# Two transformer blocks on one Trainium2 core: the four feed-forwards issue their TensorE products in four other forms

## The reference

```
x = layer_norm(a * x + 0.5 * swiglu_ffn(x, ffn_w_in[i, 0], ffn_w_out[i, 0]), ...)
x = layer_norm(a * x + mixer(x), ...)
x = layer_norm(a * x + memory_cross_attention(x, mem, ...), ...)
x = layer_norm(a * x + 0.5 * swiglu_ffn(x, ffn_w_in[i, 1], ffn_w_out[i, 1]), ...)

def swiglu_ffn(x, w_in, w_out):
    h = x @ w_in                  # 1024 -> 2 * 2816
    g, u = jnp.split(h, 2, axis=-1)
    return (jax.nn.silu(g) * u) @ w_out   # 2816 -> 1024
```

## Time and profile before

| | |
|---|---|
| runs shown | 3226.77, 3240.44 and 3244.69 us; median 3240.44 us |
| profiled execution | span 3246.9 us, 58680 instructions (the page states no other time of it; first to last instruction) |
| PE busy | 3078.8 us, 95% of the span, 24248 instructions |
| PEld busy | 2819.9 us, 87%, 24248 instructions |
| POOL, DVE, ACT busy | 1351.4 us (42%), 1128.6 us (35%), 1121.9 us (35%) |
| TensorE clock granted, mean | 0.974 of full |

### The profile page before, as it was taken

The page is one execution under the profiler, slowest core; times in us unless marked ns, Lnnn a source line. Parts: engine busy times, 40 slices in busy tenths (PEclk is TensorE's granted clock), DMA queues, the critical chain, the costliest instruction groups (busy, mean ns, idle before and its releaser), DMA issues.

```text
span 3246.9 us, 58680 instructions
## 1 busy us (share of the span) xinstructions
PE 3078.8 (95%) x24248; PEld 2819.9 (87%) x24248; DVE 1128.6 (35%) x1881; ACT 1121.9 (35%) x1894; POOL 1351.4 (42%) x648
## 2 busy tenths in 40 slices
PE   7998998999899999989889999999999999899998
PEld 7986588987488999979479789999999988789997
DVE  1525742534843211152760541102211054541103
ACT  4333733233733222232733332222322244332222
POOL 5434045433134444344036254444554445254443
PEclk9998999999999999999989999999999999999999
DMA  5211023212012232222013122232222332122231
GB/s 191 72 66 52 1 68 115 72 46 73 13 52 93 90 103 97 91 77 92 14 52 121 62 78 90 90 104 84 84 95 99 100 113 86 46 84 91 99 102 58
DMA packets 72059, 261.19 MB, mean 80 GB/s; under 512 B 8016, under 2 KB 8656, under 8 KB 70896
## 3 DMA queue, kind: packets, MB, share of 16 engines
q1 hardware_dynamic: 69728, 249.77, 23.0%
q10 hardware_dynamic: 2192, 9.44, 0.8%
HBM read 257.09 MB, written 2.10 MB: 80 GB/s over the span
## 4 chain that ended last, share of the span: by engine, by line
PE 86%; DVE 8%; ACT 2%; issue 2%; POOL 1%; DMA 0%; ACTq 0%; DVEq 0%; POOLq 0%
PE bank L524 25%; PE bank L506 16%; PE bank L510 16%; PE bank L508 16%; PE bank L664 1%; PE bank L837 1%; PE bank L869 1%; PE bank L853 1%; PE bank L1078 1%; DVE small L2187 1%; PE bank L1069 1%; PE bank L715 1%; POOL wl L392 1%; DVE tb L1819 1%; PE bank L907 1%
## 5 line engine op out<-in xcount | busy, mean ns | idle before, releaser
L392 POOL TENSOR_TENSOR wl<-raw,wh 128x1024 fp32r<-128x1024 f32 x464 | 1151.9, 2497 | 1794.0 <-ACT wh L1182 1793.8
L1182 ACT CAST wh<-raw 128x1024 fp32r<-128x1024 f32 x464 | 472.9, 1049 | 1035.1 <-PE bank L510 804.2
L506 PE MATMUL bank<-xh,wh 128*128 128x256 f32 x3168 | 641.6, 284 | 0.0
L508 PE MATMUL bank<-xl,wh 128*128 128x256 f32 x3168 | 625.2, 279 | 0.0
L510 PE MATMUL bank<-xh,wl 128*128 128x256 f32 x3168 | 624.9, 279 | 0.0
L506 PEld LDWEIGHTS bank<-xh,wh 128*128 128x128 f32 x3168 | 485.1, 190 | 19.7 <-issue 18.3
L508 PEld LDWEIGHTS bank<-xl,wh 128*128 128x128 f32 x3168 | 483.3, 189 | 0.0
L510 PEld LDWEIGHTS bank<-xh,wl 128*128 128x128 f32 x3168 | 483.3, 189 | 0.0
L524 PE MATMUL bank<-xh,wh 128*128 128x256 f32 x1952 | 394.9, 285 | 53.6 <-ACT xh L1244 37.6
L524 PE MATMUL bank<-xh,wl 128*128 128x256 f32 x1952 | 392.4, 283 | 0.0
L524 PEld LDWEIGHTS bank<-xh,wh 128*128 128x128 f32 x1952 | 305.6, 194 | 64.8 <-issue 64.1
(11 more groups left out here) (338 smaller groups left out, 3797.5 us busy)
## 6 DMA issues: line engine op xcount, KB each, us to landing
raw<-in_slabs SPq DMA_DIRECT2D x464, 512.0 KB, 3.3
h<-in_x_t SPq DMA_DIRECT2D x8, 256.0 KB, 5.5
w1v<-in_w ACTq DMA_DIRECT2D x2, 1024.0 KB, 5.0
side<-in_pp_w ACTq DMA_DIRECT2D x2, 1024.0 KB, 5.2
out<-h SPq DMA_DIRECT2D x8, 256.0 KB, 2.0
side<-in_w SPq DMA_DIRECT2D x1, 1024.0 KB, 12.6
vt<-in_p_t ACTq DMA_DIRECT2D x2, 512.0 KB, 6.5
side<-in_w ACTq DMA_DIRECT2D x1, 1024.0 KB, 7.2
```

Of the source, the lines that this page charges most:

```text
L392: nc.gpsimd.tensor_tensor(wl[:, n % RING, :], raw[:, n % RING, :], wh[:, n % RING, :], A.subtract).then_inc(w_low, 1)
L506: nc.tensor.matmul(dst[:, c], high_l, high_r[:, c], start=first and n == 0, stop=False)
L508: nc.tensor.matmul(dst[:, c], high_l, low_r[:, c], start=False, stop=False)
L1182: nc.scalar.copy(wh[:, slot, :], raw[:, slot, :]).then_inc(w_high, 1)
```

## The change

`columns_of` gives the cuts of a 512-column bank under four names: halves (256 + 256, as before), whole (512), wide_first (280 + 232) and wider_first (320 + 192). `passes`, `part`, `pair` and `products` take a form. The four feed-forwards get:

| feed-forward | ffn_in | ffn_out |
|---|---|---|
| (0, 0) | the first product of each `passes` pair cut 280 + 232, the rest in halves | whole |
| (0, 1) | whole | halves |
| (1, 0) | the first product of each `passes` pair cut 320 + 192, the rest in halves | `by_half`: all three products of one half, then of the other |
| (1, 1) | halves, and ahead of every pair a constant bf16 product of 128 columns into bank 7, which nothing reads | halves |

`first_form` reaches only the `passes` pair of a trip and there only the first product of chunk 0 into the first bank, so it touches 11 products of a stage. All other stages keep their halves.

```
--- before.py
+++ after.py
@@ -497,12 +497,27 @@
 
         @blk.tensor
         def _(pe):
-            def passes(dst, high_l, low_l, high_r, low_r, first, last):
-
-                w = dst.shape[1]
-                cut = w // 2 if w == T else w
-                parts = [slice(a, a + cut) for a in range(0, w, cut)]
+            def columns_of(w, form):
+
+                if w != T:
+                    return [slice(0, w)]
+                at = {"halves": (0, 256, T), "whole": (0, T), "wide_first": (0, 280, T), "wider_first": (0, 320, T)}[form]
+                return [slice(a, b) for a, b in zip(at, at[1:])]
+
+            def by_half(dst, high_l, low_l, high_r, low_r, first, last):
+
+                parts = columns_of(dst.shape[1], "halves")
                 for n, c in enumerate(parts):
+                    nc.tensor.matmul(dst[:, c], high_l, high_r[:, c], start=first and n == 0, stop=False)
+                    nc.tensor.matmul(dst[:, c], high_l, low_r[:, c], start=False, stop=False)
+                    out = nc.tensor.matmul(dst[:, c], low_l, high_r[:, c], start=False,
+                                           stop=last and n == len(parts) - 1)
+                return out
+
+            def passes(dst, high_l, low_l, high_r, low_r, first, last, form="halves", first_form=None):
+
+                parts = columns_of(dst.shape[1], form)
+                for n, c in enumerate(columns_of(dst.shape[1], first_form or form)):
                     nc.tensor.matmul(dst[:, c], high_l, high_r[:, c], start=first and n == 0, stop=False)
                 for c in parts:
                     nc.tensor.matmul(dst[:, c], high_l, low_r[:, c], start=False, stop=False)
@@ -514,18 +529,16 @@
             def tile_of(n, j):
                 return wh[:, n % RING, j * P:(j + 1) * P], wl[:, n % RING, j * P:(j + 1) * P]
 
-            def part(dst, terms, first, last):
-
-                w = dst.shape[1]
-                cut = w // 2 if w == T else w
-                cols = [slice(a, a + cut) for a in range(0, w, cut)]
+            def part(dst, terms, first, last, form="halves"):
+
+                cols = columns_of(dst.shape[1], form)
                 for i, (fixed, moving) in enumerate(terms):
                     for n, c in enumerate(cols):
                         out = nc.tensor.matmul(dst[:, c], fixed, moving[:, c], start=first and i + n == 0,
                                                stop=last and i == len(terms) - 1 and n == len(cols) - 1)
                 return out
 
-            def pair(slab, kind, act_h, act_l, w, high_in=None, low_in=None):
+            def pair(slab, kind, act_h, act_l, w, high_in=None, low_in=None, form="halves", first_form=None):
 
                 banks = [bank[2 * kind + o][:, 0:w] for o in range(2)]
                 for k in range(KC if low_in is None else KC + 1):
@@ -534,21 +547,23 @@
                             high_in(k)
                         for o in range(2):
                             a, b = tile_of(slab + o, k)
-                            last = passes(banks[o], a, b, act_h[:, k, :], act_l[:, k, :], k == 0, k == KC - 1)
+                            last = passes(banks[o], a, b, act_h[:, k, :], act_l[:, k, :], k == 0, k == KC - 1, form,
+                                          first_form if k + o == 0 else None)
                         continue
                     if k < KC:
                         high_in(k)
                         for o in range(2):
                             a, b = tile_of(slab + o, k)
-                            part(banks[o], ((a, act_h[:, k, :]), (b, act_h[:, k, :])), k == 0, False)
+                            part(banks[o], ((a, act_h[:, k, :]), (b, act_h[:, k, :])), k == 0, False, form)
                     if k:
                         low_in(k - 1)
                         for o in range(2):
                             a, _ = tile_of(slab + o, k - 1)
-                            last = part(banks[o], ((a, act_l[:, k - 1, :]),), False, k == KC)
+                            last = part(banks[o], ((a, act_l[:, k - 1, :]),), False, k == KC, form)
                 return last
 
-            def products(st, slab, ticket, step, pairs, split_base, act_h=xh, act_l=xl, w=T, resumed=False):
+            def products(st, slab, ticket, step, pairs, split_base, act_h=xh, act_l=xl, w=T, resumed=False,
+                         form="halves", first_form=None, touch=False):
 
                 if not resumed:
                     pe.wait_ge(took_a, ticket)
@@ -568,7 +583,10 @@
                             pe.wait_ge(took_v, i * 2 + (ticket + j - 1))
 
                         two_steps = (high_in, low_in) if split_base is not None and j == 0 else ()
-                        pair(slab + 2 * j, j, act_h, act_l, w, *two_steps).then_inc(prod, 1)
+                        if touch:
+                            nc.tensor.matmul(bank[7][:, 0:P], ident_b[:], causal_b[:], start=True, stop=True)
+                        pair(slab + 2 * j, j, act_h, act_l, w, *two_steps, form=form, first_form=first_form
+                             ).then_inc(prod, 1)
                 if pairs == 2:
                     two(0)
                 else:
@@ -927,9 +945,18 @@
                     last.then_inc(prod, 1)
 
             def ffn_in(st):
-                products(st, st["slab"], st["took"], st["prod"], NF, st["xl"] - KC)
+                how = {(0, 0): dict(first_form="wide_first"), (0, 1): dict(form="whole"),
+                       (1, 0): dict(first_form="wider_first"), (1, 1): dict(touch=True)}[st["layer"], st["which"]]
+                products(st, st["slab"], st["took"], st["prod"], NF, st["xl"] - KC, **how)
 
             def ffn_out(st):
+
+                at = (st["layer"], st["which"])
+
+                def one_product(*a):
+                    if at == (1, 0):
+                        return by_half(*a)
+                    return passes(*a, "whole" if at == (0, 0) else "halves")
 
                 def one(slab, k_h, k_l, first):
                     for o in (4, 5, 6, 7, 0, 1, 2, 3):
@@ -938,7 +965,7 @@
                             pe.wait_ge(took_a, st["took"] - 1 + o // 2)
                             pe.wait_ge(took_v, st["took"] - 1 + o // 2)
                         a, b = tile_of(slab, o)
-                        last = passes(bank[o][:], a, b, k_h, k_l, first, False)
+                        last = one_product(bank[o][:], a, b, k_h, k_l, first, False)
                     last.then_inc(prod, 1)
                 for k in range(TAIL):
                     pe.wait_ge(w_low, st["slab"] + k + 1)
@@ -956,7 +983,7 @@
                 for o in range(KC):
                     for k in range(NF - TAIL, NF):
                         a, b = tile_of(st["slab"] + k, o)
-                        last = passes(bank[o][:], a, b, hh[:, k, :], hl[:, k, :], False, k == NF - 1)
+                        last = one_product(bank[o][:], a, b, hh[:, k, :], hl[:, k, :], False, k == NF - 1)
                     if o % 2:
                         last.then_inc(prod, 1)
 

```

## The result

The changed kernel took 3250.76 us (median of 18 runs, 3244.96 to 3258.21) against 3236.16 us for the kernel before (18 runs, 3224.19 to 3255.01), a ratio of 1.0046 with a 95% interval of 1.003 to 1.0063. It is slower by 14.6 us, where 3225 us had been forecast. (That sum was made on the span; the time of a run, as listed, is about 1.9 us longer than its span.) The spread says something of its own: before, the runs lie 31 us apart, with the change 13 us.

The account below looks back on a forecast made before the run. The prediction took TensorE, busy 95% of the span, as the bound, set by how far apart its instructions start. Its terms summed to -21.7 us on the span of 3246.9, making 3225 us, range 3210 to 3258.

Parts of the forecast that it names:

- Term 1: ffn_in of (0, 1) in whole banks: 1056 products at 220 ns, -16.5 us (ends -21.1 and -4.8).
- Rival B: Whole products no cheaper than their halves, the excess growing with columns: 3242 us at 231 ns; chance 0.19.
- Term 2: ffn_out of (0, 0) whole: 474 products at 220 for 226.7 ns, -3.2 us (ends -5.2 and +2.2).
- Term 3: ffn_out of (0, 1), unchanged halves: pace drawn anew behind whole products, fast, -4.2 us (ends -4.2 and 0).
- Term 4: ffn_in of (0, 0) and (1, 0), 11 uneven first products each: 0 us if the pace holds.
- Rival A: Uneven and bf16 products throw fast stages into the slow pace: 3262 to 3266 us, one stage 3235 to 3239; chance 0.25.
- Term 5: ffn_out of (1, 0) by half: the same instructions and weight loads, 0 us.
- Term 6: ffn_in of (1, 1), 22 bf16 products at 100 ns: +2.2 us (ends +1.3 and +4.4).
- Rival C: The gain only luck, as (0, 1) is fast anyway in the executions compared: -8.1 on the median, 3232 us; chance 0.13.

Follow-up runs that it names:

- the kernel with one entry exchanged: Changed kernel with ffn_in of (0, 0) cut 320 + 192 in place of 280 + 232; 3243.94 us, ratio 1.0017 to the kernel before.

## Why the prediction was wrong

**Term 1 failed, by its size and its sign.** It priced a whole product at 220 ns, the fast pace's excess taken once, "because the excess of fp32r products ... shows no growth with columns". The row beside that sentence, 280 columns at 126.4 ns, and its own upper end of 231 ns were the better guide: the whole product costs 233.3 ns. 1056 x 233.3 = 246.4 us against 248.8 at the slow pace is -2.4 us in place of -16.5, and against a fast stage it is +7.0 us. The f32 product of the same moving time was the wrong neighbour, and the rule of the Trainium skill ("TensorE: Matmul & The Clock Gate", Back-to-back issue gap) that went with it, N / 2.4 + 2.5 ns, misses fp32r by 17.5 ns at 512 columns. That section gives the formula for products standing alone, not for a stream as the prediction has it, and the f32 rows of 256 columns agree with it only if each column is counted twice. Rival B had the mechanism, given 0.19; its time was 3242 us.

**Term 2** fell with the same price: 474 x 6.7 = +3.2 us, not -3.2. (By its own 231 ns the high end is +2.0, not +2.2.) That the tail gives nothing back the traces bear out: from the first product of (0, 0)'s `ffn_out` to its last it is 119.57 us before and 122.97 with the change, 3.40 more, but to the last product of the layer norm's statistics 124.25 and 127.41, only 3.16 more.

**Term 3** held: (0, 1)'s `ffn_out` came fast behind whole products, -4.2 us, in the changed kernel's profile and in that of the kernel with one entry exchanged.

**Term 4 failed at (0, 0).** "0 us if the pace holds" was left as the likely case because fast halves stood behind 280-column products. A run of 96 such products and a single one ahead of 232 columns are not the same thing. The single one sets the slow pace: 10.5 trips x 0.86 = +9.0 us. Rival A had the mechanism, with chance as its law; one stage was thrown, for which it gave 3235 to 3239 us, and by its cut, not by luck. 320 + 192 cost 11 x 0.05 = 0.5 us and left its stage fast.

**Term 5** held, 0 us. **Term 6** was 11 x 0.31 = 3.4 us for 2.2, inside its ends.

Sum of the terms as measured: -2.4 + 3.2 - 4.2 + 9.0 + 0.5 + 3.4 = +9.5 us on the profiled execution, which would be 3256.4; the 5.4 us won ahead of the first feed-forward leave 3251.0, 0.7 under the 3251.7 measured.

**The base was the third fault.** The sum took the profiled (0, 1), which was slow, for the usual one. The runs say otherwise. From the kernel with 320 + 192 alone, four fast feed-forwards make 3232.4 - 2 = 3230.4 us. On that base the change is 9.0 + 3.2 + 7.0 + 0.5 + 3.4 = +23.1, 3253.5 us (measured 3250.8); the bf16 products everywhere +13.6, 3244.0 (3243.9); whole everywhere 4 x 10.2, 3271.2 (3270.2); 280 + 232 everywhere 4 x 13.2, 3283.2 (3283.0); and the changed kernel without 280 + 232 +14.6, 3245.0 (3243.9). The medians of before, 3236 to 3243, lie 6 to 13 us above the base, so by this estimate half a feed-forward to one of the four is slow. The thirteen profiles agree: of the 42 `ffn_in` stages that open with halves, 8 open slow, which is 0.8 of four. Rival C, "the gain was only luck", belonged into the forecast's own arithmetic. That the time lies in the range of 3210 to 3258 us is no merit of the sum: the time is 26 us above it, in the room left for rivals A and B, a part of each of which came true. By the prediction's own bound of 0.5% the ratio of 1.0046 is no change, but its interval lies wholly on the slower side, away from the forecast. The narrower spread of the changed kernel fits: at most the first pair of (0, 0), (1, 0) and (1, 1) still has a drawn pace, and whole products have none.

## What to carry to other kernels

Where TensorE bounds a kernel, divide its busy time by its count, stage by stage: two paces in equal code at the same granted clock are a state of the stream, and a profile shows one draw of it. An edit in such a kernel is costed against both states, with their frequency from several executions, not against the one that the profile caught. And a price for a new width is taken from rows of the same data type, even few and far ones, ahead of rows of another type that happen to have the same duration.

## What the runs showed of the hardware

- fp32r products of 256 columns with a weight load each run at 113.3 or 117.8 ns, start to start, both at the full granted clock, and hold either for thousands of instructions. Which one a feed-forward begins with is drawn by the time that the clock has risen (8 of 42 slow); a single unlike product then sets, keeps or turns it as in the table above, but for 320 + 192 in the first trip of a stage that began slow, which set the fast pace in two of four.
- The distance grows faster than the columns at 2.4 GHz: 280 columns 126.4 ns (9.7 over), 512 columns 233.3 ns (20 over), while the sums for 320 + 192, 384 + 128 and 448 + 64 fit one full place of near 113 ns and the wide part's columns with their excess (worked out). From start to start the wide part takes 168, 227 and 286 ns and the narrow one 90, 58 and 29.
- The same cut acts otherwise in another stream: 320 + 192 does not set the fast pace in the token-major products, where the activations are the stationary operand and the bank changes every two or four halves (0 of 26); 256 + 128 + 128 does with `xh` and `xl` (3 of 3), and with `mh` and `ml` does not (0 of 8). Why the paces exist, and what in the array or its reads of SBUF makes a cut set or turn them, stays open; no run here separates the two.
